# Second mixer: the sums of the log terms along the keys as four fp32r matmuls for each head, and those of heads 2 and 3 one quarter later

## What is computed

```python
def stick_breaking(q, k, v):
    ...
        z = jnp.einsum('bthd,bshd->bhts', qb, k).astype(jnp.float32) * d_h ** -0.5
        ...
        mask = key_pos[None, :] < t_pos[:, None]
        lo = jnp.where(mask, jax.nn.log_sigmoid(-z), 0.0)
        rc = lax.cumsum(lo, axis=3, reverse=True)
        log_a = jax.nn.log_sigmoid(z) + (rc - lo)
        a = jnp.where(mask, jnp.exp(log_a), 0.0)
        return jnp.einsum('bhts,bshd->bthd', a.astype(v.dtype), v)
```

## Time and profile before

| | us |
|---|---|
| median of 3 runs | 995.01 (994.93 to 995.31) |
| the profiled execution | 995.19 |
| its span, first to last instruction | 993.4 |
| outside the span | 1.8 |
| PE busy with matmuls | 982.2 |
| DVE busy | 622.8 |
| ACT busy | 534.7 |

### The profile page before, as it was taken

One profiled execution on the slowest core, in us unless ns is written; L12 is line 12 of the kernel. 1 busy time (PEld: TensorE's weight loads), 2 busy tenths in 40 slices (PEclk: granted clock), 3 DMA queues, 4 the chain that ended last, 5 costly groups with the idle time before them and its releaser, 6 DMA issues.

```text
span 993.4 us, 15044 instructions
## 1 busy us (share of the span) xinstructions
PE 982.2 (99%) x6318; PEld 884.5 (89%) x6318; DVE 622.8 (63%) x830; ACT 534.7 (54%) x770; POOL 239.2 (24%) x76
## 2 busy tenths in 40 slices
PE   9999999999999999999999999999999999999997
PEld 7888889999888788889999888899899999999885
DVE  4997956788412554546888321477447689888543
ACT  6676346545333477846555433454554687665532
POOL 0021045566565000015566565400000000000000
PEclk9999999999999999999999999999999999999999
DMA  8454224554555544334554555454443535554531
GB/s 334 171 190 149 85 89 167 181 200 171 200 181 188 192 155 144 128 131 170 181 201 170 187 194 175 177 196 147 167 170 128 212 121 198 192 190 170 199 140 43
DMA packets 24807, 168.51 MB, mean 170 GB/s; under 512 B 2781, under 2 KB 3092, under 8 KB 4900
## 3 DMA queue, kind: packets, MB, share of 16 engines
q1 hardware_dynamic: 24452, 167.22, 47.1%
q10 hardware_dynamic: 288, 0.33, 0.1%
HBM read 166.49 MB, written 1.05 MB: 169 GB/s over the span
## 4 chain that ended last, share of the span: by engine, by line
PE 92%; ACT 3%; DVE 2%; issue 1%; DMA 1%; SPq 0%; DVEq 0%; ACTq 0%
PE bank L650 28%; PE bank L651 28%; PE bank L652 28%; PE bank L850 2%; ACT whi L1153 2%; DVE wlo L1712 1%; PE bank L678 1%; DMA raw<-w_stream 1%; PE bank L818 0%; PE bank L867 0%; PE bank L1061 0%; PE bank L1045 0%; PE bank L960 0%; PE bank L886 0%; PE bank L950 0%
## 5 line engine op out<-in xcount | busy, mean ns | idle before, releaser
L1712 DVE TENSOR_TENSOR wlo<-raw,whi 128x2048 fp32r<-128x2048 f32 (+2 forms) x152 | 280.4, 1845 | 268.7 <-ACT whi L1153 268.6
L1153 ACT ACTIVATE whi<-raw 128x2048 fp32r<-128x2048 f32 (+1 forms) x154 | 292.6, 1901 | 158.1 <-PE bank L652 152.1
L2374 POOL TENSOR_TENSOR wlo<-raw,whi 128x1024 fp32r<-128x1024 f32 (+1 forms) x69 | 238.1, 3451 | 396.2 <-ACT whi L1153 388.8
L650 PE MATMUL bank<-nhi,whi 128*128 128x256 f32 (+3 forms) x832 | 238.4, 287 | 0.0
L651 PE MATMUL bank<-nlo,whi 128*128 128x256 f32 (+3 forms) x832 | 235.5, 283 | 0.0
L652 PE MATMUL bank<-nhi,wlo 128*128 128x256 f32 (+3 forms) x832 | 235.1, 283 | 0.0
L650 PEld LDWEIGHTS bank<-nhi,whi 128*128 128x128 f32 (+1 forms) x832 | 158.2, 190 | 3.7 <-issue 3.6
L651 PEld LDWEIGHTS bank<-nlo,whi 128*128 128x128 f32 (+1 forms) x832 | 158.3, 190 | 0.2
L652 PEld LDWEIGHTS bank<-nhi,wlo 128*128 128x128 f32 (+1 forms) x832 | 158.3, 190 | 0.0
L650 PE MATMUL bank<-mhi,whi 128*128 128x258 f32 x384 | 109.2, 284 | 0.0
L651 PE MATMUL bank<-mlo,whi 128*128 128x258 f32 x384 | 108.4, 282 | 0.0
(11 more groups left out here) (292 smaller groups left out, 1573.6 us busy)
## 6 DMA issues: line engine op xcount, KB each, us to landing
raw<-w_stream SPq DMA_DIRECT2D x154, 1024.0 KB, 4.8
cst<-consts SPq DMA_DIRECT2D x1, 1200.0 KB, 11.5
h<-x_rows SPq DMA_DIRECT2D x4, 256.0 KB, 5.5
raw<-w_stream SPq DMA_DIRECT2D x2, 512.0 KB, 6.5
out_rows<-e SPq DMA_DIRECT2D x4, 256.0 KB, 2.1
e<-g_post SPq DMA_DIRECT2D x1, 512.0 KB, 3.3
raw<-w_stream SPq DMA_DIRECT2D x1, 352.0 KB, 9.6
b<-consts_x SPq DMA_DIRECT2D x1, 272.0 KB
```

The source lines that it names most:

```text
L650: pe.matmul(out, lhsT.hi, rhs.hi, start=start, stop=False)
L1153: act.activation(whi[j][:, 0:n], raw[j][:, 0:n], ACT.Copy).then_inc(s_hi.up(i))
L1712: dve.tensor_tensor(wlo[j][:, 0:m], raw[j][:, 0:m], whi[j][:, 0:m].bitcast(F32), ALU.subtract).then_inc(s_lod.up(i))
L2374: pool.tensor_tensor(wlo[j][:, m:n], raw[j][:, m:n], whi[j][:, m:n].bitcast(F32), ALU.subtract).then_inc(s_lop.up(i))
```

## The change

`key_sums` took the log terms in fp32: three matmuls (256, 128 and 128 columns), two of them with a triangle of ones `tri` and one with a square of ones. It now takes them as a pair of fp32r tiles, high and low part, and makes four fp32r matmuls (384, 384, 128 and 128 columns) with the same masks in fp32r (`later`, `every`, made once by two copies on ACT). The pair is made for each head by a new copy on ACT (`sum_hi`, 128x384, over the second buffer of `ZB[head]`) and a new subtraction on DVE (`sum_lo`, 128x384, over the third). The steps `sr 2` and `sr 3` move from behind quarters 0 and 1 of projection 10 to behind quarters 1 and 2, `sr 3` ahead of `cT 3`. The order in which banks are given out stays the same.

```diff
-    (10, 0): [("sr", 2)],
-    (10, 1): [("sr", 3)],
-    (10, 2): [("cT", 3)],
+    (10, 1): [("sr", 2)],
+    (10, 2): [("sr", 3), ("cT", 3)],
...
-        ZB = [[A(384) for _ in range(3)] for _ in range(NZ)]
+        ZB, LP = [], []
+        for hd in range(NZ):
+            o = A.at
+            ZB.append([A(384) for _ in range(3)])
+            LP.append(Pair(at(f"lhi{hd}", 384, o + 4 * 384, F32R), at(f"llo{hd}", 384, o + 8 * 384, F32R)))
+        later, every = A(P, F32R), A(P, F32R)
...
             def key_sums(hd):
-                LL = ZB[hd][2]
-                u = begin("sr", hd)
-                on.wait_ge(*s_sll.at(hd))
-                pe.matmul(u.t[:, 0:256], tri, LL[:, 0:256], start=True, stop=False)
-                pe.matmul(u.t[:, P:256], ones, LL[:, 256:384], start=False, stop=True)
-                pe.matmul(u.t[:, 256:384], tri, LL[:, 256:384], start=True, stop=True).then_inc(u.full)
+                L, u = LP[hd], begin("sr", hd)
+                on.wait_ge(*s_mask.at(1))
+                on.wait_ge(*s_lllo.at(hd))
+                pe.matmul(u.t[:, 0:384], later, L.hi, start=True, stop=False)
+                pe.matmul(u.t[:, 0:384], later, L.lo, start=False, stop=False)
+                pe.matmul(u.t[:, P:256], every, L.hi[:, 256:384], start=False, stop=False)
+                pe.matmul(u.t[:, P:256], every, L.lo[:, 256:384], start=False, stop=True).then_inc(u.full)
...
+            def sum_hi(hd):
+                on.wait_ge(*s_sll.at(hd))
+                act.activation(LP[hd].hi, ZB[hd][2], ACT.Copy).then_inc(s_llhi.up(hd))
...
             hi(C0 + 5)
+            on.wait_ge(*TC)
+            act.activation(later, tri, ACT.Copy).then_inc(s_mask.up(0))
+            act.activation(every, ones, ACT.Copy).then_inc(s_mask.up(1))
             turn(0, 0)
...
             log_term(1)
+            sum_hi(0)
             normed(2)
+            sum_hi(1)
             hi(C0 + 8)
...
             log_term(3)
+            sum_hi(2)
             normed(3)
+            sum_hi(3)
             hi(C0 + 10)
...
             values(0)
+            sum_hi(4)
             log_term(5)
             hi(C0 + 12)
             log_term(6)
+            sum_hi(5)
             shares(4)
+            sum_hi(6)
             log_term(7)
             cat_hi(1, "sv", 0)
             shares(5)
             hi(C0 + 13)
             cat_hi(1, "sv", 1)
+            sum_hi(7)
             shares(6)
...
+            def sum_lo(hd):
+                on.wait_ge(*s_llhi.at(hd))
+                dve.tensor_tensor(LP[hd].lo, ZB[hd][2], LP[hd].hi.bitcast(F32), ALU.subtract).then_inc(s_lllo.up(hd))
...
             log_sum(1)
+            sum_lo(0)
             normed(2)
+            sum_lo(1)
             lo(C0 + 8)
...
             log_sum(3)
+            sum_lo(2)
             normed(3)
             log_share(2)
+            sum_lo(3)
             lo(C0 + 10)
...
             masked(5)
+            sum_lo(4)
             log_sum(5)
             masked(6)
             lo(C0 + 12)
             log_sum(6)
+            sum_lo(5)
             log_share(4)
             masked(7)
+            sum_lo(6)
             log_share(5)
             log_sum(7)
             cat_lo(1, "sv", 0)
             cat_lo(1, "sv", 1)
+            sum_lo(7)
             log_share(6)
             cat_lo(1, "sv", 2)
```

More of the change, by code:

```diff
@@ L614, in block_kernel @@
         s_gs, s_crs = sig("gs", [0]), sig("crs", range(8))
-        s_sln, s_sll, s_sa = (sig(n, range(8)) for n in ("sln", "sll", "sa"))
+        s_sln, s_sll, s_llhi, s_lllo, s_sa = (sig(n, range(8)) for n in ("sln", "sll", "llhi", "lllo", "sa"))
+        s_mask = sig("mask", range(2))
         s_mr, s_mn, s_mhi, s_mlo = (sig(n, [0]) for n in ("mr", "mn", "mhi", "mlo"))
```

## The result

The changed kernel takes 997.37 us in the median of 9 runs (997.07 to 999.13), the kernel before 995.16 in 9 runs on the same chip (994.93 to 995.38): a ratio of 1.0028, 95% interval 1.0019 to 1.0037 (this ratio and those below are of the means; of the medians it is 1.0022). It is slower by 2.2 us. The nine times of the changed kernel lie in two groups, five from 997.07 to 997.37 and four from 998.63 to 999.13, so the median is the highest of the lower group, whose middle is 997.18. The profiled execution took 997.37 with a span of 995.4. One execution in this study, of the kernel with the move alone, took 5389.6 us at a granted clock of 0.17, and its ratio leaves it out.

What follows compares the result with a forecast made beforehand. PE bounds the kernel (982.2 of 993.4 us), but a serial ACT and DVE chain sets the mixer's end: +1.9 us at `sv 3`, profiled 995.19 to 997.1, against the median 996.9 us; main case 996.4 to 997.5, stated range 994.8 to 998.0.

Steps and rivals of the forecast that it cites:

- Step 1: Copy 0 on ACT delays normed 2 by 0.43 us; second half of `cT 2` on PE begins at 383.70, not 383.26.
- Step 3: Copies 2 and 3 stand around normed 3 on ACT; hi(C0+10) goes from 399.75 to 401.49 us (+1.74).
- Step 4: PE reaches `sr 2`, behind quarter 1 of projection 10, at 397.3 and waits 0.5 us for sum_lo 2.
- Step 5: At `sr 3`, now ahead of `cT 3`, PE waits 1.7 us for its input; `cT 3` begins 1.55 us later.
- Step 7: sum_lo 5 on DVE stands ahead of log_share 4, so shares 4 on ACT moves from 416.83 to 419.02.
- Step 8: Copy 7 and sum_lo 7 use up ACT's 1.69 us of slack at shares 6; `sv 3` starts at 427.12, not 425.21.
- 128-column fp32r matmuls: In a head's sums on PE, taken at 0.11 us each, giving 0.57 us a head (0.46 to 0.78).
- clock: A granted clock falling in PE's 1.7 us wait at `sr 3` would make the whole forecast too low; no size given.
- main case: The tail of the ACT and DVE chain decides: +1.9 us at `sv 3`, 996.4 to 997.5 us; chance 0.60.
- B: Wait at `sr 3` happens, but slack at shares 4 and 6 hides copies 4 to 7: 995.0 to 996.2; chance 0.14.
- C: Copies on ACT start 0.55 us apart, not 0.43, six of them on the chain: +2.6 us, 997.6; chance 0.13.
- A: Copies and subtractions fall into ACT and DVE waits that nothing hangs on, PE's saving arrives: 992.2 us; chance 0.13.

## Why the prediction held, and where its sizes were off

The steps can be read off against the trace of after, with 0.17 added to it; of each pair of numbers the first is the prediction's. *Step 1*: the second half of `cT 2` at 383.70; 383.70. *Step 2*: log_term 2 at 393.04; 393.03. *Step 3*: hi(C0+10) at 401.49; 401.44. *Step 4*: a wait of 0.5 at `sr 2`; 0.66. *Step 5*: `sr 3` at 402.9 after a wait of 1.7, `cT 3` at 403.46; 402.92 after 1.55, and 403.52. *Step 6*: log_term 5 1.72 later; 1.68. *Step 7*: shares 4 at 419.02; 418.99. *Step 8*: `sr 7` near 426.0 and `sv 3` at 427.12; 425.93 and 427.02. The sum was +1.9 us; the trace has +1.8 at `sv 3`. One remark of step 8 is wrong and changes nothing in it: the 1.69 us at shares 6 are not used up, 1.09 are left, since log_share 6, which ends them, moves too.

Two terms were mis-sized. The **128-column fp32r matmuls** were taken at 0.11 us, after the transposes; they start 0.07 and 0.10 apart, near the line through 258 and 512 columns, so a head costs 0.51, not 0.57. As the prediction said, this didn't enter the end, and the run with fp32 sums shows the same from the other side. For the matmul of 128 columns the Trainium skill (TensorE: Matmul & The Clock Gate, Back-to-back issue gap) has about 81 ns, closer than what I took.

The **clock** stood among the things that would make the forecast too low, tied to the longest wait, at `sr 3`. It falls, but elsewhere: behind `sr 7` and `sv 3`, after a shorter wait. The kernel with its tail turned round keeps the wait of 1.55 us at `sr 3` and all its ten times lie within 0.5 us. So the median of 997.37 lies 0.2 above the middle of the lower group. Another 0.15 is that the forecast starts from 995.01 for the kernel before, which took 995.16 beside the changed one. These and 0.1 us that I can't place are what is missing to 996.9. In the first profile of after, 0.35 us more came in the last MLP, where its matmuls of 258 columns ran a little further apart; the later profile at 997.13 doesn't have it, so it is no part of the change.

The rivals. The stated range, 994.8 to 998.0, takes in the main case, B and C, so the time alone decides only against A; the starts and waits above decide between the others. *A*, the saving arrives, is out for the changed kernel. Its size was nearly right (992.2 worked out, 992.5 measured with the new steps on GpSimd and the tail turned round), in part by luck: the sums save 2.9 us and not 2.4, and the wait at `cT 2` grows from 0.46 to 0.8. *B*, the head binds and the tail doesn't, is what the changed kernel with the turned tail makes: 995.5, inside its 995.0 to 996.2. The tail did bind, as step 8 had it. *C*, copies at 0.55 in the queue, is out, though its 997.6 is nearer to the median of 997.37 than 996.9 is: a copy's slot is 0.42. On the question of slower or within 0.2% the prediction leaned a little to the wrong side, 0.45 for within and 0.42 for slower; the ratio is 1.0028, 1.0022 by the medians, and its interval begins at 1.0019.

What the prediction missed is the other half of its own reading. It counted PE's 0.19 at `sr 7` and 0.06 at `sv 3` as signs of the chain, but gave rival A 2.8 us as if that chain had room; the run without pairs shows that only 1 us in the median, 1.3 in its lower group, arrives without touching the tail.

## What to carry to other kernels

An engine that is busy 54% of the time has no room if its idle times are ended by another engine of the same chain: follow each idle time to what ended it, and put a new step's full length, as the distance of two starts, on everything behind it up to the next idle time that the chain doesn't end. Ask of each saving on the bound engine where it waits next; here eight savings of 0.36 us were worth 0.4 us at most in the changed kernel. With the new steps on an idle engine the kernel was some 0.7 us faster than before in the median, too little to be told from none, and 2.7 us faster when one weight tile, due 7 us later, and one other step of ACT's tail were taken out of the way as well. Put the steps that feed PE ahead of those that nobody waits for yet.

## What the runs showed of the hardware that was not expected

GpSimd rounds 128x384 to fp32r in 0.50 us, as fast as ACT (0.51), and subtracts 128x384 in 1.02, while 128x1024 took 3.45 beside DVE's part of the same tile. And behind waits of PE of 1.24 and 0.33 us, 0.76 us apart, the granted clock fell to its lower level for some 3 us in one of two further profiles of the changed kernel, and by the times in about half of its executions.

The other kernels bear this out by their times. Where a wait of 1.2 us or more at `sr 7` is followed by 0.33 at `sv 3`, the times lie in two groups, 0.8 us or more apart: the changed kernel (4 of 9 in the upper group), the one without pairs (4 of 10), the one with pairs on GpSimd (4 of 10) and the one with `cT 3` first (5 of 7). Each execution of an upper group has a granted clock of 0.996 or 0.997 over the span, each of a lower group 0.998 or 0.999. The four changed kernels without these two waits have no upper group in 33 executions, though the one with only the tail turned round keeps its wait of 1.55 us at `sr 3`. Whether it is the two waits together or the work around them that decides was not tried.
